# Key product of the experts with the two halves of the activations side by side: one 512-column matmul in place of two of 256

## The reference, cut to what matters

```
h = rms_norm(x, norm_ffn[l])                       # 256 tokens x 1024
s1, i1 / s2, i2 = top 16 of 128 sub-keys, twice    # per token and head
eidx, gate = the 16 best sums, softmax of them
act = gelu(einsum('td,ted->te', xb, u[eidx])) * gate
x = x + einsum('te,ted->td', act, v[eidx])
```

## Time and profile before

| | us |
|---|---|
| median of 3 executions (2449.44 to 2452.45) | 2451.8 |
| span of the profiled execution | 2449.8 |
| PE busy in it | 2230.3 (91%) |
| PEld busy | 2005.3 (82%) |
| DVE busy | 1488.7 (61%) |
| ACT busy | 1184.6 (48%) |
| POOL busy | 638.2 (26%) |

### The profile page before, as it was taken

How to read it: one execution, slowest core, us unless ns; L and a number is a source line. 1 busy time by engine, 2 the same in 40 slices (tenths; PEclk the granted TensorE clock), 3 DMA queues, 4 the chain that set the end, 5 groups by cost and what they waited for, 6 DMA issues and landing times.

```text
span 2449.8 us, 45057 instructions
## 1 busy us (share of the span) xinstructions
PE 2230.3 (91%) x14560; PEld 2005.3 (82%) x14560; DVE 1488.7 (61%) x2872; ACT 1184.6 (48%) x2597; POOL 638.2 (26%) x712
## 2 busy tenths in 40 slices
PE   8789899799997699999897898998999976999997
PEld 7788599799996578888787885997999965788886
DVE  5853369844447766666658533697444477666665
ACT  4630254355457755555545202543444577555554
POOL 6522029600006810000065120395000078000000
PEclk9899899999999999999988988999999999999999
DMA  5210344345551045555542103443455400455555
GB/s 216 93 52 1 112 148 170 135 159 186 180 179 52 0 143 199 190 190 193 190 176 86 35 1 133 146 168 127 167 186 185 175 34 0 165 195 188 191 198 185
DMA packets 47450, 338.70 MB, mean 138 GB/s; under 512 B 5648, under 2 KB 5776, under 8 KB 6928
## 3 DMA queue, kind: packets, MB, share of 16 engines
q1 hardware_dynamic: 47376, 337.73, 38.5%
HBM read 336.66 MB, written 1.05 MB: 138 GB/s over the span
## 4 chain that ended last, share of the span: by engine, by line
PE 73%; DVE 20%; issue 3%; ACT 2%; DMA 1%; POOL 0%; DVEq 0%; SPq 0%; ACTq 0%; PEldq 0%; POOLq 0%
PE ps L771 10%; PE ps L770 10%; PE ps L769 10%; PE ps L746 7%; PE ps L747 7%; PE ps L748 7%; PE ps L758 4%; DVE big L1489 2%; PE ps L650 2%; DVE big L1529 2%; PE ps L380 2%; PE ps L382 2%; PE ps L381 2%; PE ps L514 2%; DVE big L1488 1%
## 5 line engine op out<-in xcount | busy, mean ns | idle before, releaser
L746 PE MATMUL ps<-h_t_hi,expert_hi 128*128 128x256 f32 x2048 | 589.1, 288 | 38.2 <-POOL expert_lo L1628 16.9
L747 PE MATMUL ps<-h_t_lo,expert_hi 128*128 128x256 f32 x2048 | 582.1, 284 | 0.0
L748 PE MATMUL ps<-h_t_hi,expert_lo 128*128 128x256 f32 x2048 | 581.7, 284 | 0.0
L746 PEld LDWEIGHTS ps<-h_t_hi,expert_hi 128*128 128x128 f32 x2048 | 395.3, 193 | 51.4 <-issue 30.5
L1507 DVE TENSOR_TENSOR expert_lo<-w_ring,expert_hi 128x512 fp32r<-128x512 f32 x368 | 237.9, 688 | 299.7 <-ACT expert_hi L933 299.6
L769 PE MATMUL ps<-expert_hi,act_hi 128*128 128x512 f32 x1024 | 399.6, 390 | 4.6 <-DVE act_lo L1515 4.6
L771 PE MATMUL ps<-expert_hi,act_lo 128*128 128x512 f32 x1024 | 399.8, 390 | 0.0
L770 PE MATMUL ps<-expert_lo,act_hi 128*128 128x512 f32 x1024 | 399.6, 390 | 0.0
L748 PEld LDWEIGHTS ps<-h_t_hi,expert_lo 128*128 128x128 f32 x2048 | 395.7, 193 | 0.0
L747 PEld LDWEIGHTS ps<-h_t_lo,expert_hi 128*128 128x128 f32 x2048 | 395.6, 193 | 0.0
L1511 DVE TENSOR_TENSOR expert_lo<-w_ring,expert_hi 128x512 fp32r<-128x512 f32 x512 | 331.3, 688 | 0.4
(11 more groups left out here) (288 smaller groups left out, 3686.8 us busy)
## 6 DMA issues: line engine op xcount, KB each, us to landing
w_ring<-u_t SPq DMA_DIRECT2D x128, 1024.0 KB, 4.8
w_ring<-v_t SPq DMA_DIRECT2D x128, 1024.0 KB, 4.8
w_ring<-w_in SPq DMA_DIRECT2D x32, 1024.0 KB, 4.9
w_ring<-w_q SPq DMA_DIRECT2D x16, 1024.0 KB, 4.8
w_ring<-w_out SPq DMA_DIRECT2D x8, 1024.0 KB, 4.8
big<-xconst SPq DMA_DIRECT2D x2, 1666.0 KB, 9.5
w_ring<-keys SPq DMA_DIRECT2D x2, 1024.0 KB, 4.8
big<-rows SPq DMA_DIRECT2D x2, 576.0 KB, 11.3
```

What stands on the lines that cost most here:

```text
L746: pe.matmul(o, w_hi[:, c, :], HTH[:, d, :], start=d == 0, stop=False)
L747: pe.matmul(o, w_hi[:, c, :], HTL[:, d, :], start=False, stop=False)
L748: mm = pe.matmul(o, w_lo[:, c, :], HTH[:, d, :], start=False, stop=d == DC - 1)
```

## The change

`HTH` and `HTL` become the two halves of one tensor `HTP`, channel chunk by channel chunk, so that 512 columns of high and low lie side by side. Bodies 0 to 8 go on as they are. In bodies 9 to 31 the two products with the high weight become one matmul over 512 columns into a whole PSUM bank, whose left half holds high by high and whose right half holds high weight by low activation. The product with the low weight is added into the left half as before. The two halves of the bank are added by DVE, in a reduction over pairs, into banks 6 and 7; gelu reads them there. PE's wait for a free bank becomes a wait for that addition; gelu's wait for PE becomes a wait for it too. DVE's additions stand in its program where gelu stands in ACT's, after `u_lows(m)` for m = 1, 3, 5, 7.

```diff
-        HTH = sb("h_t_hi", [P, DC, S], F32R)
-        HTL = sb("h_t_lo", [P, DC, S], F32R)
+        HTP = sb("h_t_pair", [P, DC, 2, S], F32R)
+        HTH, HTL = HTP[:, :, 0, :], HTP[:, :, 1, :]
...
+            def u_wide(m, j, first):
+
+                e, f = m // 2, m % 2
+                pe.wait_ge(u_lo, 8 * (j - POOL_BODIES) + m + 1)
+                if f == 0:
+                    if first and e < 2:
+                        pe.wait_ge(u_act, 4 * j + e - 1)
+                    else:
+                        pe.wait_ge(u_sum, 4 * (j - POOL_BODIES) + e - 1)
+                w_hi = EH[:, m % 4, :].rearrange("p (c n) -> p c n", c=4)
+                w_lo = EL[:, m % 4, :].rearrange("p (c n) -> p c n", c=4)
+                both = PS[:, 4 + e % 2, :].rearrange("p (a n) -> p a n", a=2)
+                for c in range(4):
+                    d = 4 * f + c
+                    if d < DC - 1:
+                        pe.matmul(both, w_hi[:, c, :], HTP[:, d, :, :], start=d == 0, stop=False)
+                        mm = pe.matmul(both[:, 0, :], w_lo[:, c, :], HTH[:, d, :], start=False, stop=False)
+                    else:
+                        pe.matmul(both[:, 0, :], w_lo[:, c, :], HTH[:, d, :], start=False, stop=False)
+                        mm = pe.matmul(both, w_hi[:, c, :], HTP[:, d, :, :], start=False, stop=True)
                 mm.then_inc(u_done, 1)
...
+            def u_gelu_wide(e, j):
+
+                act.wait_ge(u_sum, 4 * (j - POOL_BODIES) + e + 1)
+                act.activation(ACTS[:, 4 * j + e, :], PS[:, 6 + e % 2, 0:S], ACT.Gelu).then_inc(u_act, 1)
...
+            def u_body_wide(j, first):
+                for m in range(8):
+                    u_split(m, j, False)
+                    if m == 1:
+                        if first:
+                            u_gelu(-1, j)
+                        else:
+                            u_gelu_wide(-1, j)
+                    if m >= 3 and m % 2:
+                        u_gelu_wide(m // 2 - 1, j)
...
                 for i in range(3):
                     gate_rows(i, i, True)
-                u_gelu(-1, N_BODY)
+                u_gelu_wide(-1, N_BODY)
...
+            def u_sums(e, j):
+
+                dve.wait_ge(u_done, 8 * j + 2 * e + 2)
+                dve.wait_ge(u_act, 4 * j + e - 1)
+                dve.tensor_reduce(PS[:, 6 + e % 2, 0:S], PS[:, 4 + e % 2, :].rearrange("p (a n) -> p n a", a=2), AX.X, ALU.add).then_inc(u_sum, 1)
+
+            def u_body(j, first):
+                for m in range(8):
+                    u_lows(m, j)
+                    if m == 1 and not first:
+                        u_sums(-1, j)
+                    if m >= 3 and m % 2:
+                        u_sums(m // 2 - 1, j)
...
                 with dve.Fori(GATE_BODY, N_BODY) as j:
-                    for m in range(8):
-                        u_lows(m, j)
+                    u_body(j, False)
+                u_sums(-1, N_BODY)
                 dve.wait_ge(sel_out, 3)
                 for i in range(3):
                     hots(i, i, True)
```

More of the change, by code:

```diff
@@ L264, in trunk @@
         u_hi, u_lo, u_done, u_act = sem("u_hi"), sem("u_lo"), sem("u_done"), sem("u_act")
+        u_sum = sem("u_sum")
         hot_eq, hot_gate, hot_pool, quad_done, quad_out = (sem(n) for n in ("hot_eq", "hot_gate", "hot_pool", "quad_done", "quad_out"))
@@ L724, in turn_sel, with u_half @@
                     mm.then_inc(sel_done, 1)
-            def u_half(m, j, first, pool):
+            def u_half(m, j, first):
                 e, f = m // 2, m % 2
[L731 to L734, removed]
+                pe.wait_ge(u_lo_pool, 8 * j + m + 1)
                 if f == 0:
@@ L748, in u_half @@
                     mm = pe.matmul(o, w_lo[:, c, :], HTH[:, d, :], start=False, stop=d == DC - 1)
+                mm.then_inc(u_done, 1)
+            def u_wide(m, j, first):
[17 more added lines that the diff above has]
+                        mm = pe.matmul(both, w_hi[:, c, :], HTP[:, d, :, :], start=False, stop=True)
                 mm.then_inc(u_done, 1)
@@ L829, in _ @@
                 for m in range(8):
-                    u_half(m, 0, True, True)
+                    u_half(m, 0, True)
                 pe.sem_inc(passed, 1)
@@ L833, in _ @@
                     for m in range(8):
-                        u_half(m, j, False, True)
-                with pe.Fori(POOL_BODIES, SEL_BODY) as j:
+                        u_half(m, j, False)
+                for m in range(8):
+                    u_wide(m, POOL_BODIES, True)
+                with pe.Fori(POOL_BODIES + 1, SEL_BODY) as j:
                     for m in range(8):
-                        u_half(m, j, False, False)
+                        u_wide(m, j, False)
                 turn_sel()
@@ L1116, in _ @@
                 act.sem_inc(passed, 1)
-                with act.Fori(1, EXP_BODY) as j:
+                with act.Fori(1, POOL_BODIES) as j:
                     u_body(j, False)
+                u_body_wide(POOL_BODIES, True)
                 act.wait_ge(gdiff_ready, 1)
                 act.activation(GATE[:, :, :], GATE[:, :, :], ACT.Exp).then_inc(gexp_ready, 1)
-                u_body(EXP_BODY, False)
+                u_body_wide(EXP_BODY, False)
                 with act.Fori(EXP_BODY + 1, SEL_BODY) as j:
-                    u_body(j, False)
+                    u_body_wide(j, False)
                 pair = IDXQ[:, :, :].rearrange("p q (m t) -> p m q t", m=2)
@@ L1574, in _ @@
                 dve.sem_inc(passed, 1)
-                with dve.Fori(POOL_BODIES, GATE_BODY) as j:
-                    for m in range(8):
-                        u_lows(m, j)
+                u_body(POOL_BODIES, True)
+                with dve.Fori(POOL_BODIES + 1, GATE_BODY) as j:
+                    u_body(j, False)
                 gates()
                 with dve.Fori(GATE_BODY, N_BODY) as j:
-                    for m in range(8):
-                        u_lows(m, j)
+                    u_body(j, False)
+                u_sums(-1, N_BODY)
                 dve.wait_ge(sel_out, 3)
```

## The result

| | us, median | ratio to before, 95% interval |
|---|---|---|
| before (4 executions) | 2452.1 | |
| changed (4 executions, 2474.8 to 2481.4) | 2479.1 | 1.0111 (1.0097 to 1.0126) |

The kernel became slower by 1.1%; 2480 us was forecast. The profiled execution of it has a span of 2479.6 us, 29.8 over that of before.

A forecast was written before the change was run, and what follows sets the result against it. PE bounds the kernel before; after the change a ring of ACT and DVE does. +19.8 - 0.4 + 1.7 + 7.2 = +28.3 on the span of 2449.8, plus 2.0 for timed runs: 2480 us; range 2452 to 2514.

The forecast's parts named there:

- The ring: Bodies 9 to 31: addition, gelu, split, low parts wait in turn on ACT and DVE; 2.955 us a block, +19.8 us.
- The addition: DVE's sum of 512 PSUM elements into 256 in each block: 0.685 us, with ends of 0.41 and 0.953.
- The rivals with a short or a long addition: DVE's addition: 0.50 or less, 2440 us (13%); about 0.55, 2455 us (10%); 0.953, 2529 us (15%).
- The stage as a whole: Bodies 9 to 31, both layers: ring +19.8 us, PE's lead -0.4, exponential in body 10 +1.7.
- the six transposes: Ahead of body 14: a serial passage through PE, ACT, DVE and PE in both versions, costing nothing.
- A seam: Between two bodies on ACT: 0.13 us added to four turns, making a body 11.95 us.
- PE's lead: First block of body 9 still has it: -0.2 us for each layer, -0.4 us in all.
- the gate sums ahead of body 11: On DVE: 1.2 us that fit while ACT does gelu and the first split, costing nothing.
- The hand-over of 0.13: In each turn, from the end of DVE's addition to the start of ACT's gelu: 0.13 us.
- The end of the stage: Last addition stands ahead of hots on DVE, so gated(0) starts later: +3.6 us each layer, +7.2 in all.
- PE's gain: Wide matmul in bodies 9 to 31: a chunk takes 0.3464 us, not 0.360; 20.0 us if PE sets the pace.
- PE keeps the pace: Rival, bodies 9 to 31: a turn falls under PE's 2.77 us and its 20.0 us come; 2440 us, 13%.

The follow-up runs named there:

- e1: Changed kernel with gelu one split later in ACT's program, same instructions; 2441.7 us, ratio to before 0.9963.
- e4: Changed kernel with the addition over the first 128 tokens only, lasting 0.431 us; 2436.8 us, ratio to before 0.9948.
- e9: Changed kernel with the addition done twice, the first time into unused columns; 2581.2 us, ratio to before 1.0555.
- e2: Changed kernel with the wide matmul split again into two of 256 columns, addition and waits kept; 2475.8 us, ratio to before 1.0112.
- e6: Changed kernel with ACT's loops over bodies 11 to 13 and 14 to 31 written out; 2456.1 us, ratio to before 1.0024.
- e3: Changed kernel without the addition: wide matmul kept, gelu reads the bank's left half and waits for PE; 2436.2 us, ratio to before 0.993.
- e5: Changed kernel with a layer's last addition moved behind the first three quads' hots in DVE's program; 2470.8 us, ratio to before 1.0083.
- e8: Changed kernel with the moves of e1 and e5, and each half's matmuls sorted into four wide and four narrow; 2432.2 us, ratio to before 0.9939.
- e10: Changed kernel with the moves of e1 and e5, and the low-weight matmul 512 columns wide too; 2584.5 us, ratio to before 1.0569.

## Why the prediction was right

**The ring: right, shown.** Every step came out within 0.01 us: 0.65, 1.21, 0.69, 0.13, 0.28; the turn 2.96 against 2.955. That it sets the pace, and not PE or DVE's total, is shown from four sides: another order of the same instructions removes the loss (e1), a shorter addition too (e4), a longer one adds its own length in each turn (e9), and PE's matmuls don't matter behind it (e2).

**The addition: right.** 0.692 us against 0.685. The rivals with a short or a long addition fall with it.

**The stage as a whole: 1.5 us a layer too high, and mostly for a reason in the kernel before.** From the first low part to PE's last matmul it was 282.3 us against 273.3 (759.57 - 477.26, 748.69 - 475.40), +9.0, where 9.9 - 0.2 + 0.87 = 10.6 was forecast. Piece by piece, from the first low part of a body to that of another (layer 1; layer 2 agrees within 0.1):

| bodies | before | after | difference | forecast |
|---|---|---|---|---|
| 9 to 11 | 24.6 | 26.4 | +1.7 | +1.5 |
| 11 to 13 | 23.3 | 24.0 | +0.7 | +0.9 |
| 13 to 15 | 27.9 | 27.1 | -0.8 | +0.9 |
| 15 to 31 | 184.3 | 192.1 | +7.8 | +6.9 |
| 31 to PE's last matmul | 13.2 | 12.8 | -0.4 | +0.4 |

The largest miss, 1.7, lies where the six transposes stand, which the prediction put at nothing as a serial passage in both versions. The passage is the same: PE is idle 2.44 us in both. But behind it, in body 14 of the kernel before, the granted clock fell from 1.0 to 0.50, from the 2.4 GHz level to that of 1.2, for some 3.4 us, and matmuls of 256 columns started 0.214 apart in place of 0.120:

```profile
539.60 0.38 PE L746 MATMUL ps<-h_t_hi,expert_hi 128*128 128x256 f32 x1 [2.44 <-ACT big L938]
...
541.03 0.42 PE L748 MATMUL ps<-h_t_hi,expert_lo 128*128 128x256 f32 x1
...
543.81 0.41 PE L746 MATMUL ps<-h_t_hi,expert_hi 128*128 128x256 f32 x1
```

Two windows in body 14, of the kernel before and then of the changed one (the clock is third from the end):

```profile
541.00:544.00 3.00, 3.00 (x16) 3.00 (x15) 0.44 (x1) 0.00 (x0) 2.32 (x5) 0.50 0.46 85
545.00:548.00 3.00, 3.00 (x19) 2.50 (x18) 1.90 (x3) 1.45 (x5) 2.75 (x4) 1.00 0.00 0
```

Seventeen starts take 3.54 us there (540.88 to 544.42) in place of 2.04, so PE, which sets the pace, lost 1.5; layer 2 has the same fall at 1759.5. The profiled execution of the changed kernel keeps 1.0 in both layers. The fall is not a matter of the change: e6 has it in both layers, e1 in layer 2 alone (where the stage is 266.8 us, against 265.5), e2 and e3 in neither, with the same 2.44 us of idle PE in e3. What decides it is open. Without it the stage would be 10.5 us longer than before, so the forecast of 10.6 was right for a kernel without the fall, and the profile cannot tell how often the timed executions have it.

The rest are small errors that cancel. A seam costs 0.16, not 0.13 (12.00 a body against 11.95: +0.9 over bodies 15 to 30). At the end of the stage PE no longer lags behind the low parts as it did: 12.82 - 12.00 = 0.8 us in place of 13.20 - 11.52 = 1.7, where the prediction took 0.2 for PE's lead. And in bodies 9 to 11 two things oppose each other: the gate sums ahead of body 11, priced at nothing, delay the low parts by some 0.4, while bodies 9 and 10 stand outside a loop and turn in 2.86, not 2.96:

```profile
495.81 0.69 DVE L1552 TENSOR_REDUCE ps<-ps 128x256 f32<-128x512 f32 x1
...
496.54 0.39 ACT L965 ACTIVATE big<-ps 128x256 f32<-128x256 f32 x1 [1.45 <-DVE ps L1552]
...
499.40 0.39 ACT L965 ACTIVATE big<-ps 128x256 f32<-128x256 f32 x1 [1.45 <-DVE ps L1552]
```

Here gelu comes 0.04 after the addition's end. The hand-over of 0.13 was taken from a row inside a loop, and used for all.

**The end of the stage: right**, +3.4 for +3.6; e5 shows the cause in DVE's order.

**The quads: not foreseen.** They take 2.1 us a layer more, with programs that the change doesn't touch. Over the ten experiments they take from 114.8 to 119.3 us, with no order by the length of the stage ahead: 117.0 in e8, 119.2 in e2, 114.8 in e4 and in e9. Four engines wait for each other there, and the length may depend on how they enter. A rival is the clock: its mean over the quads is 0.99 in the kernels with 114.8 us, 0.96 before and 0.94 and 0.93 after. But 0.90 and 0.98 in the two layers of e1 go with 118.9 and 117.9 us, and 0.94 and 0.99 in those of e8 both with 117.0, so the clock alone does not order them either. Both are argued, not shown; the cause is open.

**The total: closer than its parts, by luck.** The layers took 14.3 and 14.4 us more, against 28.3 for both in the forecast. The stage came 1.5 us a layer under the forecast, for the fall of the clock in the kernel before, and the quads' 2.1, not foreseen, made up for it.

**PE's gain: mis-sized, with no effect here.** The prediction's 0.2264 + 0.120 = 0.3464 a chunk was 0.3525, so that the 20.0 us of the rival "PE keeps the pace" are 11.0. The two prices came from streams of one size each. In a mixed stream the pair costs 6 ns more; the all-wide stream has 0.227 (e10), and the sorted one gives about half of it back (0.349, e8). PE's block is then 2.82 us, so the gap that it has in each turn is 0.14 us, and not the 0.18 that the prediction named as a sign.

## What to carry to other kernels

A step added to an engine that even then has 38% of its time free can still set the pace, if it stands between two steps of another engine's in-order program: draw the turn (who waits for whose last result, in program order) and compare its length with the bound, before comparing busy shares. Such a ring can be opened by moving one waiting instruction behind an independent one on the same queue; here this turned a loss of 1.1% into a gain of 0.4% (0.6% with the end of the stage and PE's order mended too). Prices of instructions taken from a uniform stream, or from inside a loop, are off by some per cent in a mixed stream, or outside of it. And before a microsecond or two is put down to a change, compare the granted clock of the stretch in both profiles: here a fall in the kernel before hid 1.5 us a layer.

## What the runs showed of the hardware

- ACT's gelu starts 0.13 us (0.15 at a seam) after the end of DVE's addition inside a hardware loop, where waits and addresses come from a register, and 0.03 to 0.04 us after it outside of one, where they are constants: turns of 2.96 and 2.86 us for the same work (e6).
- A reduction by DVE of pairs 1 KB apart, from PSUM into PSUM, takes 0.692 us for 512 elements (0.699 in the order of e1), as much as an operation on 512 elements side by side (0.685 to 0.688).
- On PE, fp32r matmuls of 256 columns start 0.120 apart and those of 512 columns 0.227; in turn they take 0.3525 the pair, not 0.347 (e3, e10).
- After 2.44 us of idle PE the granted clock fell to 0.50 for some 3.4 us in the kernel before and in e6, and stayed at 1.0 after the same idle time in the changed kernel and in e3.
